# Paged attention over a compressed key-value cache: each group's page request issued in four quarters of the tokens

## The reference

```python
ckv_past = cache_ckv[l, page_table].reshape(db, past_len, KV_LORA)      # 8 sequences x 64 pages x 128 tokens x 256
kr_past = cache_krope[l, page_table].reshape(db, past_len, MLA_ROPE)    # the same tokens x 32
...
q_lat = jnp.einsum('bthn,lhn->bthl', q_nope, w_uk)
s_past = (jnp.einsum('bthl,bpl->bhtp', q_lat, ckv_past)
          + jnp.einsum('bthr,bpr->bhtp', q_rope, krope_past))
...
p = jax.nn.softmax(s, axis=-1).astype(c_kv.dtype)
lat = (jnp.einsum('bhtp,bpl->bthl', p[..., :P], ckv_past)
       + jnp.einsum('bhts,bsl->bthl', p[..., P:], c_kv))
```

## Time and profile before

| | us |
|---|---|
| median of 3 runs | 1907.12 (1905.14 to 1908.0) |
| the profiled execution | 1910.69 |
| its span from first to last instruction | 1908.8 |
| busy: PE / PEld | 1827.8 / 1587.6 |
| busy: DVE / ACT / POOL | 1216.4 / 569.3 / 567.0 |
| the gathers' queue (software_dynamic) | 75.50 MB in 7168 packets |

### The profile page before, as it was taken

The page is one execution under the profiler, slowest core; times in us unless marked ns, Lnnn a source line. Parts: engine busy times, 40 slices in busy tenths (PEclk is TensorE's granted clock), DMA queues, the critical chain, the costliest instruction groups (busy, mean ns, idle before and its releaser), DMA issues.

```text
span 1908.8 us, 34292 instructions
## 1 busy us (share of the span) xinstructions
PE 1827.8 (96%) x14782; PEld 1587.6 (83%) x14782; DVE 1216.4 (64%) x1563; ACT 569.3 (30%) x978; POOL 567.0 (30%) x392
## 2 busy tenths in 40 slices
PE   7999999898998999989998899999999999999998
PEld 6989889885664444449997699999999999999998
DVE  5587776565877887874332756873675276375475
ACT  5222321353553454452121531120111021011026
POOL 2222122240001343422224533333332333333530
PEclk9999999998999999999999999999999999999999
DMA  7121122141002888853134511112111211211202
GB/s 245 45 57 45 47 57 45 39 123 48 1 1 91 324 320 314 315 188 104 30 89 143 177 56 45 46 39 61 45 41 42 63 39 34 61 45 43 79 23 92
DMA packets 162307, 176.72 MB, mean 93 GB/s; under 512 B 21982, under 2 KB 146932, under 8 KB 157772
## 3 DMA queue, kind: packets, MB, share of 16 engines
q1 hardware_dynamic: 146240, 93.54, 16.7%
q0 software_dynamic: 7168, 75.50, 10.5%
q10 hardware_dynamic: 8750, 5.49, 1.0%
HBM read 161.33 MB, written 13.27 MB: 91 GB/s over the span
## 4 chain that ended last, share of the span: by engine, by line
PE 87%; DVE 7%; issue 3%; ACT 1%; DMA 1%; POOL 1%; SPq 0%; ACTq 0%; DVEq 0%; POOLq 0%
PE PS L799 21%; PE PS L801 20%; PE PS L800 20%; PE PS L1120 4%; PE PS L836 4%; PE PS L1162 3%; PE PS L1014 2%; PE PS L1107 1%; PE PS L1142 1%; PE PS L1055 1%; PE PS L1131 1%; PE PS L881 1%; PE PS L987 1%; PE PS L1335 1%; PE PS L1337 1%
## 5 line engine op out<-in xcount | busy, mean ns | idle before, releaser
L737 POOL CAST whi<-wraw 128x1024 fp32r<-128x1024 f32 (+4 forms) x142 | 137.4, 968 | 915.8 <-PE PS L801 860.0
L799 PE MATMUL PS<-BH,whi 128*128 128x344 f32 x1152 | 368.9, 320 | 0.0
L800 PE MATMUL PS<-BL,whi 128*128 128x344 f32 x1152 | 367.1, 319 | 0.0
L801 PE MATMUL PS<-BH,wlo 128*128 128x344 f32 x1152 | 367.0, 319 | 0.0
L739 POOL TENSOR_TENSOR wlo<-wraw,whi 128x1024 fp32r<-128x1024 f32 (+4 forms) x142 | 311.2, 2192 | 11.4
L800 PEld LDWEIGHTS PS<-BL,whi 128*128 128x128 f32 x1152 | 216.2, 188 | 0.5 <-issue 0.5
L799 PEld LDWEIGHTS PS<-BH,whi 128*128 128x128 f32 x1152 | 216.2, 188 | 0.5 <-issue 0.5
L801 PEld LDWEIGHTS PS<-BH,wlo 128*128 128x128 f32 x1152 | 216.2, 188 | 0.0
L799 PE MATMUL PS<-XH,whi 128*128 128x344 f32 x528 | 179.0, 339 | 3.4 <-DVE XL L1911 3.4
L2391 DVE TENSOR_TENSOR XT<-PS,XT 128x1032 f32<-128x1032 f32 x48 | 59.2, 1233 | 175.9 <-PE PS L801 175.8
L800 PE MATMUL PS<-XL,whi 128*128 128x344 f32 x528 | 170.1, 322 | 0.0
(11 more groups left out here) (451 smaller groups left out, 3713.5 us busy)
## 6 DMA issues: line engine op xcount, KB each, us to landing
wraw<-in_w_up_dram SPq DMA_DIRECT2D x44, 512.0 KB, 3.9
wraw<-in_w_in_dram SPq DMA_DIRECT2D x20, 512.0 KB, 4.0
wraw<-in_w_down_dram SPq DMA_DIRECT2D x24, 256.0 KB, 2.9
wraw<-in_w_down_dram SPq DMA_DIRECT2D x16, 320.0 KB, 3.3
xt_kept<-XT SPq DMA_DIRECT2D x1, 4128.0 KB, 12.8
XT<-xt_kept SPq DMA_DIRECT2D x1, 4128.0 KB, 13.9
xstage<-in_x_prompt_dram SPq DMA_DIRECT2D x8, 512.0 KB, 10.4
wraw<-in_w_out_dram SPq DMA_DIRECT2D x8, 512.0 KB, 4.2
```

Of the source, the lines that this page charges most:

```text
L737: gp.tensor_copy(hi, raw).then_inc(w_hi_done, 1)
L799: pe.matmul(out, wh[:, t, 0:m], hi[:, tile(t), s], start=(t == first), stop=False)
L800: pe.matmul(out, wh[:, t, 0:m], low, start=False, stop=False)
L801: ins = pe.matmul(out, wl[:, t, 0:m], hi[:, tile(t), s], start=False, stop=(t == last))
```

## The change

The view of `cache_ckv` is cut into rows of 4 tokens (4 KB) where it had rows of 16 tokens (16 KB). `load_pages` issues the request for `rk` first and then four for `rc`, each for four of the 16 tokens of every partition, all directly behind each other. All five add to the same `page_in` semaphore, and DVE waits for 80 where it waited for 32. Four more index tiles are made at the start: page number times 32 plus 4 * (p % 8) + n. The buffers hold the same data at the same places as before, and the computation on them is not touched. All tiles that are allocated behind the index tile move up by the new tiles' size.

```diff
+        PARTS = 4
         idx = keep("idx", [P, GT], I32)
+        idx_part, row_part = [keep(f"idx_part{n}", [P, GT], I32) for n in range(PARTS)], keep("row_part", [P, PARTS])
...
-            ckv_rows = i["cache_ckv"][0].rearrange("n (a t) l -> (n a) (t l)", t=GP)
+            ckv_rows = i["cache_ckv"][0].rearrange("n (a t) l -> (n a) (t l)", t=GP // PARTS)
...
-                at_ = bass.IndirectOffsetOnAxis(ap=idx[:, g:g + 1].bitcast(U32), axis=0)
-                for dst, rows in ((rc, ckv_rows), (rk, kr_rows)):
-                    gp.indirect_dma_start(out=dst[g % SLOTS][:, :, :].rearrange("p t l -> p (t l)"), out_offset=None, in_=rows,
-                                          in_offset=at_).then_inc(page_in[g % SLOTS], 16)
+                request(g, rk, kr_rows, idx, 0, GP)
+                for part in range(PARTS):
+                    load_part(g, part)
+
+            def load_part(g, part):
+                request(g, rc, ckv_rows, idx_part[part], part * GP // PARTS, (part + 1) * GP // PARTS)
+
+            def request(g, dst, rows, rows_at, t0, t1):
+                at_ = bass.IndirectOffsetOnAxis(ap=rows_at[:, g:g + 1].bitcast(U32), axis=0)
+                gp.indirect_dma_start(out=dst[g % SLOTS][:, t0:t1, :].rearrange("p t l -> p (t l)"), out_offset=None,
+                                      in_=rows, in_offset=at_).then_inc(page_in[g % SLOTS], 16)
...
+            for n in range(PARTS):
+                step(ve.tensor_scalar(row_part[:, n:n + 1], rowof[:, 0:1], float(PARTS), float(n), ALU.mult, ALU.add))
+                ve.tensor_scalar(idx_part[n][:, :], bank("idx")[:, 0:GT], 8.0 * PARTS, row_part[:, n:n + 1], ALU.mult, ALU.add)
             take(ve.tensor_scalar(idx[:, :], bank("idx")[:, 0:GT], 8.0, rowof[:, 0:1], ALU.mult, ALU.add))
...
-                ve.wait_ge(page_in[g % SLOTS], 32 * (g // SLOTS + 1))
+                ve.wait_ge(page_in[g % SLOTS], 80 * (g // SLOTS + 1))
```

## The result

The changed kernel takes 2065.63 us (median of 4 runs, 2058.32 to 2068.65), the kernel before 1907.56 us beside it: a ratio of 1.082, with a 95% interval of 1.0799 to 1.084. The forecast of no change, 1907.5 us, is wrong, and the time lies outside its range of 1893 to 1930. The profiled execution of the changed kernel has a span of 2063.0 us, 154.2 more than before.

The account below looks back on a forecast made before the run. TensorE was taken to pace the stage: profiled 1910.7 us + 0.4 (sums) + 0 (requests, transfers, start, TensorE) = 1911.1, less 3.6 for the median of runs, gave 1907.5 us. The 8-in-10 range was 1893 to 1930 us.

Parts of the forecast that it names:

- What bounds the kernel: Stage with the gathers: TensorE sets the pace, POOL idles, and pages arrive over 8 us early, so faster fetches gain nothing.
- the transfers: DMA gathers: demand of 314 GB/s stays below the 388 to 422 GB/s of similar loads; booked at 0.
- the start: Eight small DVE operations at the start, 1.9 us in all, hidden behind DVE's idle time; booked at 0.
- The requests on POOL: POOL's issuing: 0.94 us each, 1.25 start to start; three more cost 3.75 us a group, covered by its waits; booked at 0.
- The sums and who waits for them: POOL's sums start 3.75 us later, delaying ACT's copy, the exponential and TensorE: +0.4 us in all, at most 3.5.
- The floor that I gave for POOL: POOL's requests and six sums from 608.1 us on end at 820.1, limiting any gain from a shorter run to 17 us.
- What TensorE feels: L1120's long run beside the requests: disturbed by about 1.2 us in 27 groups already, unchanged by the edit; booked at 0.
- The prediction's own sign: L1120's long run in groups 2 to 28: expected 3.0 us; near 1.9 or above 3.6 us would prove the forecast wrong.
- my upper bound of 3 x 0.6 x 27 = 49 us: TensorE's long run: each of three more requests costs as much as one of the present two, in 27 groups.
- More requests, more disturbance: L1120's long run and L1131: requests disturb by number, not bytes; 1923 us with one more felt, 1956 with three; chance 0.28.
- The long run gets shorter: L1120's long run: a smaller first request, rk, disturbs TensorE less; 13 us gained, 1894.5 us; chance 0.25.
- The quarters are not overlapped: Gathers of rc: each quarter pays its own start, a group takes 13.8 us, 2069 us; transfers as bound, above 1940, chance 0.05.

Follow-up runs that it names:

- e3: Kernel before with rk asked for whole and rc in four requests of 32 partitions each, 16 KB rows (five requests a group): 2055.28 us, ratio 1.0781.
- f1: The changed kernel unaltered, run again in a job where the kernel before took 1885.03 us: 1897.26 us, ratio 1.0062.
- e7: Kernel before with rk's request left out from group 5 on (one request a group, old rope keys reused): 1883.5 us, ratio 0.988.
- e4: Kernel before with its two requests issued later, after slice 6 of TensorE's scores two groups on, and sums ahead of them: 1889.77 us, ratio 0.9916.
- e2: Kernel before with rc asked for whole and rk in quarters of the tokens, 512-byte rows (five requests a group): 2024.15 us, ratio 1.062.
- e1: Kernel before with only the order changed, rk's request issued ahead of rc's: 1906.86 us, ratio 1.0004.
- g2: Changed kernel with TensorE's waits and reports in the long run merged and a sequence's sums ahead of the five requests: 2053.24 us, ratio 1.0738.
- e5: Changed kernel with rc in two parts instead of four, 8 KB rows (three requests a group): 1952.8 us, ratio 1.0246.
- e8: As e4, but POOL waits for slice 2 of the scores instead of slice 6, so requests start about 1 us earlier: 1931.63 us, ratio 1.0134.

## Why the prediction was wrong

**What bounds the kernel, the transfers, the start.** Right: TensorE sets the stage's pace, and the pages came earlier than needed, in the changed kernel even more so (14 us for 8). Eight more operations on DVE at the start don't show.

**The requests on POOL.** Right in size: 0.94 us, 1.25 from start to start, 128 + 32 of them. That a request is "priced by its 128 rows" was wrong: in e3 one of 32 rows takes 0.86 us. In the stage the requests for rc spread over 937 to 950 ns and those for rk over 948 to 993, so there is no sign of the wait for a shared port that the Trainium skill describes (SBUF — State Buffer, "SBUF: two separate sides"). It ties that wait to certain forms of DVE's operations, and no run shows whether the ones here are among them.

**The sums and who waits for them.** Out of play in the profiled execution, since a period of 12.9 us leaves POOL time enough. In a quiet job it is this term that counts, and there it was under-sized. A period without sums is 6.5 us there, POOL needs 29.1 us for four groups of 26, so it hardly waits (4.5 us for L1171 in 7 waits), and the chain that I priced at 0.4 us in all appears at its full length. The timeline of f1 behind the sums of a sequence:

```profile
684.47 0.73 POOL L717 TENSOR_TENSOR Oacc<-Og 128x256 f32<-128x256 f32 x1
685.23 0.38 ACT L1646 ACTIVATE Og<-PS 128x256 f32<-128x256 f32 x1 [3.84 <-POOL Oacc L717]
685.51 0.68 ACT L1691 ACTIVATE Ps<-PS,dsm 128x512 f32<-128x512 f32 x1
...
686.34 0.66 PE L845 MATMUL PS<-ident,Ps 128*128 128x128 f32 x4 [1.02 <-ACT Ps L1691]
```

The copy of the values waits for the sums, the exponential stands behind the copy, and TensorE waits for the exponential. ACT's wait is 28.1 us in 6 sequences, and the kernel is 0.6% slower than the one before there. The floor that I gave for POOL, 820.1 us for the last request's end, came out: 820.2 in f1. Whether the order of POOL's work or its amount costs those 12 us wasn't tried in a quiet job.

**What TensorE feels.** This is the step that failed: "I take 0, because what the run meets in its first 2 us is alike before and after". In place of that 0 there were +113 us in the scores of groups 2 to 28, 12 us up to group 1 and 33 us at the lower clock behind the scores. The prediction's own sign came true: a run above 3.6 us (7.3). Two things were wrong in the step. First, the two requests were taken to share the 1.2 us that they cost, 0.6 each; e7 shows that the first costs nothing and the second all of it, so my upper bound of 3 x 0.6 x 27 = 49 us should have been 3 x 1.25 x 27 = 101. The clock wasn't in the step at all; it added 33 us. Second, I held the run's length fixed when I asked which requests it meets. A run that is slowed stays longer beside the requests and so meets them all; in the changed kernel the requests end before the run does, so they never got to the full-height matmuls. That these "are not disturbed" was too strong as well: e4 shows 0.45 us on L1143. The rows that I had would have carried this: the run was 1.2 us longer and a request is 1.25 us, and the earlier trace rows had no group with one request to justify halving it.

**The rivals.** "More requests, more disturbance" had the mechanism and the deciding point ("by their number and not by their bytes"), and e2 and e3 bear it out; its 1923 to 1956 us were too small for the reason above. "The long run gets shorter" is refuted by e1. "The quarters are not overlapped" came to 2069 us, near the measured 2065.6, by luck: its mechanism isn't there, the data were 14 us early. The Trainium skill's advice of 1 MiB or more in a DMA (DMA: Bandwidth & Descriptors, "Measured (HBM→SBUF, 128 partitions, SWDGE, issued from GpSimd)") would also have spoken against the quarters, but for another reason; in this trace the loss isn't in the transfers that the page speaks of.

## What to carry to other kernels

When a trace shows a stretch of one engine disturbed by another's instructions, the price is of overlap, not of an instruction: ask how long the two lie beside each other once the slowed one has grown, and let that be the upper bound. Count GpSimd's requests and look at their spacing, not only at their bytes: here three more of them for each group, for data that nobody waited for, cost 8% in disturbed jobs and 0.6% in a quiet one, and shifting the two that there were by a few us (with the sums ahead of them) won 0.8% in a disturbed one. Look at the granted clock behind a slowed stretch too. And run the two kernels side by side in every comparison: the kernel before alone differed by 1.2% between jobs.

## What the runs showed of the hardware that I had not expected

- In the disturbed jobs, around a series of indirect DMAs that POOL issues back to back, TensorE's matmuls on a quarter of the rows go on in steps of about 0.7, 1.4 or 2.1 us, whether a request has 32 or 128 rows; a lone request costs nothing. Matmuls of full height (L1143 in e4) lose 0.45 us where these lose 1.2. The Trainium skill (SBUF — State Buffer, "SBUF: two separate sides") says that PE never waits on anyone at SBUF's ports. The trace shows TensorE slowed but not at which port, so it neither bears this out nor refutes it. Whether it is the weight load, the read of the moving data, the write to PSUM or the supply of instructions is open. Late 16 KB packets on the queue "instruction" are not enough to explain it: from 640 to 980 us the changed kernel has 28 of them, and 143 slow steps.
- Behind long slowed stretches the granted clock often falls: behind the scores it is under 1.00 in 15 of 27 groups of the changed kernel (6.80 us of scores) and behind each of the six scores of 12.1 to 12.2 us in g2, but in no group of e5 (4.03 us) and of before (2.62). The length of the scores isn't all of it, since e8 has the lower clock in 10 groups with scores of 1.40 to 1.41 us.
- The slowing is there in some jobs and not in others, for the same two kernels: 1907 and 2065 us, or 1884 and 1897. The requests take the same 0.94 us in both, with the same 1.25 us from start to start.
- A second disturbance looks like one of TensorE's instruction stream. In e7 the scores of groups 2 to 10 start 6.27 to 6.30 us apart, as without any request. Some later groups have a hole in the weight loads that wanders through the program from group to group, up to 2.4 us long, and it ends 1.3 to 1.6 us after a 16 KB packet on the queue "instruction". Group 15 of e7, the long run with a hole in it:

```profile
711.21 2.53 PE L1120 MATMUL PS<-KPT,qlatR 32*8 32x512 f32 x44
```

The packet runs from 710.27 to 711.16, the hole ends at 712.7. That late instructions are the cause is argued from these times only.
